# Two layer-norm halves beside the memory panels: the order of squares, outputs and weight splits changed

## The reference

```
h = _layer_norm_2(ALPHA * h + 0.5 * _swiglu(h, ffn1_w_gate, ffn1_w_up, ffn1_w_down), ln1_g, ln1_b)
proj = h @ w_in                       # first weights of the mixers: "wm"
...
m = _layer_norm_2(mem, mem_ln_g, mem_ln_b)
k = m @ wk                            # needs the memory only, not h
v = m @ wv
```

## Time and profile before

| | us |
|---|---|
| median of 3 runs | 2746.39 (2744.63 to 2747.12) |
| profiled execution | 2743.56 |
| its span, first to last instruction | 2741.8 |
| PE busy | 2685.2 (98%) |
| DVE busy | 1288.1 (47%) |
| ACT busy | 1019.1 (37%) |
| POOL busy | 278.1 (10%) |

### The profile page before, as it was taken

How to read it: one execution, slowest core, us unless ns; L and a number is a source line. 1 busy time by engine, 2 the same in 40 slices (tenths; PEclk the granted TensorE clock), 3 DMA queues, 4 the chain that set the end, 5 groups by cost and what they waited for, 6 DMA issues and landing times.

```text
span 2741.8 us, 39300 instructions
## 1 busy us (share of the span) xinstructions
PE 2685.2 (98%) x16240; PEld 2339.8 (85%) x16240; DVE 1288.1 (47%) x2198; ACT 1019.1 (37%) x1621; POOL 278.1 (10%) x350
## 2 busy tenths in 40 slices
PE   8999999999999999999999999999999999999997
PEld 7888999999987878788888988888888887888887
DVE  4664653334442423573344543435666655633333
ACT  4654433222332223352223432323557544522222
POOL 0000300001200000220000310002211130300002
PEclk9999999999999999999999999999999999999999
DMA  3111243222121212232222232222321212232320
GB/s 141 55 47 47 78 139 110 86 93 78 47 64 61 97 60 82 93 109 93 99 93 97 77 117 92 89 96 70 111 90 62 83 64 87 88 111 93 100 70 31
DMA packets 67682, 232.93 MB, mean 85 GB/s; under 512 B 9008, under 2 KB 11440, under 8 KB 67120
## 3 DMA queue, kind: packets, MB, share of 16 engines
q1 hardware_dynamic: 67504, 230.41, 25.5%
HBM read 228.25 MB, written 2.10 MB: 84 GB/s over the span
## 4 chain that ended last, share of the span: by engine, by line
PE 87%; DVE 4%; ACT 3%; POOL 2%; issue 2%; DMA 1%; SPq 0%; DVEq 0%; POOLq 0%; ACTq 0%
PE ps L595 76%; PE ps L898 2%; PE ps L1027 1%; POOL R L2725 1%; PE ps L605 1%; PE ps L797 1%; POOL S L2710 1%; PE ps L757 1%; PE ps L885 1%; ACT HT L1275 1%; DVE HT L1948 1%; DVE R L1955 1%; PE ps L1103 1%; PE ps L1124 1%; ACT HH L1236 0%
## 5 line engine op out<-in xcount | busy, mean ns | idle before, releaser
L595 PE MATMUL ps<-XH,WH 128*128 128x264 f32 (+2 forms) x1856 | 537.8, 332 | 13.2 <-POOL SCR L2760 7.8
L595 PE MATMUL ps<-XH,LENT 128*128 128x512 f32 (+2 forms) x2096 | 527.9, 342 | 3.1 <-DVE XL L1972 2.9
L595 PE MATMUL ps<-XL,WH 128*128 128x264 f32 (+2 forms) x1856 | 522.8, 324 | 0.0
L595 PE MATMUL ps<-XH,WL 128*128 128x264 f32 (+2 forms) x1856 | 522.2, 323 | 0.0
L595 PE MATMUL ps<-HH,LENT 128*128 128x264 f32 (+2 forms) x2220 | 490.7, 319 | 1.9 <-DVE LENT L1921 1.9
L1921 DVE TENSOR_TENSOR WL<-RAW,WH 128x1024 fp32r<-128x1024 f32 (+1 forms) x232 | 284.6, 1227 | 255.3 <-ACT WH L1231 255.2
L595 PEld LDWEIGHTS ps<-XH,LENT 128*128 128x128 f32 x2096 | 356.8, 189 | 53.3 <-DVE XL L1972 4.3
L595 PEld LDWEIGHTS ps<-HH,LENT 128*128 128x128 f32 x2220 | 361.3, 190 | 32.0 <-DVE LENT L1921 2.3
L595 PEld LDWEIGHTS ps<-XH,WH 128*128 128x128 f32 x1856 | 318.7, 189 | 56.8 <-issue 13.5
L595 PEld LDWEIGHTS ps<-XH,WL 128*128 128x128 f32 x1856 | 318.2, 189 | 28.1
L595 PEld LDWEIGHTS ps<-XL,WH 128*128 128x128 f32 x1856 | 318.3, 189 | 26.6
(11 more groups left out here) (222 smaller groups left out, 2670.3 us busy)
## 6 DMA issues: line engine op xcount, KB each, us to landing
RAW<-in_wf SPq DMA_DIRECT2D x128, 512.0 KB, 3.3
RAW<-in_wr SPq DMA_DIRECT2D x48, 512.0 KB, 3.3
RAW<-in_wg SPq DMA_DIRECT2D x44, 512.0 KB, 3.3
RAW<-in_wu SPq DMA_DIRECT2D x44, 512.0 KB, 3.3
RAW<-in_wd SPq DMA_DIRECT2D x32, 512.0 KB, 3.3
RAW<-in_we SPq DMA_DIRECT2D x24, 512.0 KB, 3.3
RAW<-in_wm SPq DMA_DIRECT2D x24, 512.0 KB, 3.2
RAW<-in_wro SPq DMA_DIRECT2D x16, 512.0 KB, 3.3
```

The costliest lines, as they stand in the source:

```text
L595: mm = e.matmul(o[:, to:to + m], wt, xt[:, k, c0 + a * m:c0 + (a + 1) * m], start=(n == 0 and j == 0), stop=(n == nk - 1 and j == 2))
```

## The change

It touches only `ln1`, the norm beside memory's panels. ACT and DVE get a function `norm_pair` that lays out both halves together; POOL's order is written to match, PE's places of total, stat and bcast are moved.

1. After the reciprocal of half 0, ACT and DVE run 8 steps instead of 5, so that one more residual (wd12 6) stands ahead of `mem_to_h`; behind `mem_to_h` one weight split is made instead of up to two, and then the last residual (wd12 7).
2. The centring and squares of half 1 come next, ahead of all outputs of half 0. Their first square stands after 2 steps of memory's panels instead of 16, and 2 steps instead of 1 follow each square.
3. The outputs of half 0 go to two free tiles of `TMP` (four places) instead of `HT`, since `HT` now holds half 1's squares. ACT issues two of them ahead of half 1's root, DVE three ahead of half 1's reciprocal. The remaining outputs of half 0 and then all of half 1 follow, each with 3 steps.
4. PE asks for half 1's total after 8 steps of memory's panels instead of 16, for its stat after 20 more instead of 17; the spread follows after 3 more, as before. Half 0's bank of the spread is kept until half 1's is given back.
5. POOL adds both halves' squares and all sums ahead of the outputs.

The core of the diff (the rest passes the functions along):

```diff
@@ -527,7 +527,14 @@
 
     def first_steps(ln, half):
 
-        return (6, 16 if ln == "ln1" else 8)[half]
+        return (6, 8)[half]
+
+    def normed_tile(ln, half, k, T):
+
+
+        if (ln, half) == ("ln1", 0):
+            return TMP[:, 2 + k % 4 // 2, HALF * (k % 2):HALF * (k % 2) + T]
+        return HT[:, T_SLOT[k], 0:T]
 
     def lead_turns(ln, half):
 
@@ -650,11 +657,15 @@
             w.wait_ge(*S.const["one"])
             e.matmul(o[:, 0:T], PART[:, :], sums, start=True, stop=True).then_inc(*S.total(ln, half))
             beside_mem = ln in ("ln1", "mem")
-            pump(17 if beside_mem else 18)
+            pump(20 if (ln, half) == ("ln1", 1) else 17 if beside_mem else 18)
             rstd((ln, half), [(HT[:, 1, 0:T], S.add_pool[(ln, half, 4)]), (HT[:, 2, 0:T], S.add_dve[(ln, half, 7)])],
                  T, (S.normed, ln, half, 7), pump, 3 if beside_mem else 4)
+            if (ln, half) == ("ln1", 0):
+                return
             pump(9)
             give(("bcast", (ln, half)))
+            if ln == "ln1":
+                give(("bcast", (ln, 0)))
 
...
+        def norm_pair(ln, T, c0, res, fill, other, meanwhile):
+
+            pump = pumping(fill)
+            norm_stats(ln, 0, T, res[0], pump, first_steps(ln, 0), normed[0])
+            pump(8)
+            meanwhile()
+            ah.upto(ah.panel + 5, 1)
+            drain(fill)
+            fill = other()
+            pump = pumping(fill)
+            norm_stats(ln, 1, T, res[1], pump, 2, None, lambda: [norm_out(ln, 0, T, c0, res[0], k, True)
+                                                                                  for k in range(2)])
+            for k in range(2, 9):
+                norm_out(ln, 0, T, c0, res[0], k, True)
+                pump(3)
+            for k in range(9):
+                norm_out(ln, 1, T, c0 + T, res[1], k, True)
+                pump(3)
+            normed[0] = (ln, 1)
+            return fill
+
@@ -1273,24 +1313,22 @@
                 if k == 7:
                     w.wait_ge(*S.add_dve[ln, half, 3])
                 e.activation(HT[:, SQ_SLOT[k], 0:T], res(k), ACT.Square).then_inc(*S.sq(ln, half, k))
-                pump(1)
+                pump(2 if (ln, half) == ("ln1", 1) else 1)
             pump(3)
+            if between:
+                between()
             root((ln, half), T, inv, LN_EPS)
-            pump(5)
-            if meanwhile:
-                meanwhile()
...
@@ -1642,7 +1682,6 @@
                 w.wait_ge(*S.r_out["mem", None, k])
                 w.wait_ge(*H_free("mem"))
                 to_h("mem", k, None, mem[:, k, :], 0, 256)
-            ah.upto(ah.panel + 5)
 
         def mem_panels(a, b, beside=()):
             for name, f in MEM[a:b]:
@@ -1939,7 +1978,41 @@
             roots = WIDE[key[1] % 2][:, a:b]
             e.reciprocal(roots, roots).then_inc(*S.recip(*key, b))
 
-        def layer_norm(ln, half, T, c, res, ready, pump, first, dst, meanwhile=None):
+        def layer_norm(ln, half, T, c, res, ready, pump, first, dst):
+            norm_stats(ln, half, T, res, ready, pump, first)
+            recip((ln, half), T)
+            pump(5)
+            for k in range(9):
+                norm_out(ln, half, T, c, res, k, dst)
+                pump(3)
+            norm_done(ln, half)
+
+        def norm_pair(ln, T, c0, res, ready, fill, other, meanwhile):
+
+            pump = pumping(fill)
+            norm_stats(ln, 0, T, res[0], ready[0], pump, first_steps(ln, 0))
+            recip((ln, 0), T)
+            pump(8)
+            meanwhile()
+            ah.upto(ah.panel + 5, 1)
+            drain(fill)
+            fill = other()
+            pump = pumping(fill)
+            norm_stats(ln, 1, T, res[1], ready[1], pump, 2)
+            for k in range(9):
+                if k == 3:
+                    recip((ln, 1), T)
+                norm_out(ln, 0, T, c0, res[0], k, True)
+                if k > 1:
+                    pump(3)
+            norm_done(ln, 0)
+            for k in range(9):
+                norm_out(ln, 1, T, c0 + T, res[1], k, True)
+                pump(3)
+            norm_done(ln, 1)
+            return fill
+
+        def norm_stats(ln, half, T, res, ready, pump, first):
             def add_square(k):
 
                 w.wait_ge(*S.sq[ln, half, k])
             add_square(6)
             add_square(7)
             pump(3)
-            recip((ln, half), T)
-            pump(5)
-            if meanwhile:
-                meanwhile()
-            spread = acc(("bcast", (ln, half)), 1)[:, 0:T]
-
-            def lower(k):
-                w.wait_ge(*S.x_hi[ln, half, k])
-                sig, event = out_mark(ln, half, k)
+
+        def norm_out(ln, half, T, c, res, k, dst):
+
+            if k < 8:
+                w.wait_ge(*S.bcast[ln, half])
+                w.wait_ge(*S.centre[ln, half, k])
+                reused = k - 4 if (ln, half) == ("ln1", 0) else k - 7
+                if reused >= 0:
+                    w.wait_ge(*S.r_out[ln, half, reused])
+                    if dst:
+                        w.wait_ge(*S.x_hi[ln, half, reused])
+                e.tensor_tensor(normed_tile(ln, half, k, T), res(k), acc(("bcast", (ln, half)), 1)[:, 0:T],
+                                ALU.mult).then_inc(*S.normed(ln, half, k))
+            if k > 0 and dst:
+                w.wait_ge(*S.x_hi[ln, half, k - 1])
+                sig, event = out_mark(ln, half, k - 1)
                 w.wait_ge(*sig[event])
-                e.tensor_tensor(XL[:, k, c:c + T], res(k), XH[:, k, c:c + T].bitcast(F32),
-                                ALU.subtract).then_inc(*S.x_lo(ln, half, k))
-            for k in range(9):
-                if k < 8:
-                    w.wait_ge(*S.bcast[ln, half])
...
@@ -2738,7 +2816,16 @@
             for m in ends(0):
                 sums(*m)
             second = ends(1)
-            if ln in ("ln1", "ln4"):
+            if ln == "ln1":
+                halves_of = [lambda k, c=c0 + half * T // 2: R[:, k, c:c + T // 2] for half in (0, 1)]
+                norm_adds(ln, 0, T // 2)
+                for m in second:
+                    sums(*m)
+                norm_adds(ln, 1, T // 2)
+                norm_out(ln, 0, T // 2, halves_of[0])
+                norm_out(ln, 1, T // 2, halves_of[1])
+                return
+            if ln == "ln4":
                 between = {-1: second[0:3], 0: second[3:4], 3: second[4:5]}
             else:
```

More of the change, by code:

```diff
@@ L1257, in wide_root, with layer_norm, norm_stats @@
                          scale=inv).then_inc(*S.root(*key))
-        def layer_norm(ln, half, T, c, res, pump, first, dst, meanwhile=None):
+        def layer_norm(ln, half, T, c, res, pump, first, dst):
+            norm_stats(ln, half, T, res, pump, first, normed[0])
+            pump(5)
+            for k in range(9):
+                norm_out(ln, half, T, c, res, k, dst)
+                pump(3)
+            normed[0] = (ln, half)
+        def norm_pair(ln, T, c0, res, fill, other, meanwhile):
[17 more added lines that the diff above has]
+            return fill
+        def norm_stats(ln, half, T, res, pump, first, before, between=None):
             inv = 1.0 / 1024
@@ L1275, in layer_norm @@
                 e.activation(HT[:, SQ_SLOT[k], 0:T], res(k), ACT.Square).then_inc(*S.sq(ln, half, k))
-                pump(1)
+                pump(2 if (ln, half) == ("ln1", 1) else 1)
             pump(3)
+            if between:
+                between()
             root((ln, half), T, inv, LN_EPS)
-            pump(5)
-            if meanwhile:
-                meanwhile()
-            for k in range(9):
[L1283 to L1293, removed]
+        def norm_out(ln, half, T, c, res, k, dst):
+            if k < 8 and dst:
+                w.wait_ge(*S.normed[ln, half, k])
+                w.wait_ge(*S.panel[final(AT[X_LAST[ln]])])
+                e.activation(XH[:, k, c:c + T], normed_tile(ln, half, k, T), ACT.Identity, bias=pcol(ln + "b", k),
+                             scale=pcol(ln + "g", k)).then_inc(*S.x_hi(ln, half, k))
+            if k < 8 and out_mark(ln, half, k)[0] is S.r_act:
+                w.wait_ge(*S.normed[ln, half, k])
+                e.activation(res(k), normed_tile(ln, half, k, T), ACT.Identity, bias=pcol(ln + "b", k),
+                             scale=pcol(ln + "g", k)).then_inc(*S.r_act(ln, half, k))
         def relu2(name, idx, c0, T, half):
@@ L1382, in down_norm @@
             fill = second()
-            for half in (0, 1):
+            if meanwhile:
+                fill = norm_pair(ln, T // 2, c0, [lambda k, c=c0 + half * T // 2: R[:, k, c:c + T // 2] for half in (0, 1)], fill,
+                                 other, meanwhile)
+            for half in () if meanwhile else (0, 1):
                 if half == 1:
@@ L1389, in down_norm @@
                     ah.most = AT[LEADS[ln][-1]] + 1
```

(20 more changed lines are left out.)

18 lines of the change are left out of this document (8 added, 10 removed).

## The result

| | before | after |
|---|---|---|
| median of 22 runs each | 2745.60 us | 2748.95 us |
| lowest to highest | 2741.70 to 2747.94 | 2743.26 to 2751.14 |
| ratio, 95% interval | | 1.0012 [1.0007, 1.0018] |
| profiled execution, span | 2743.56, 2741.8 | 2749.38, 2747.6 |

What follows compares the result with a forecast made beforehand. DVE and ACT, slower than PE with outputs between splits, pace the stretch; the early total (-4.3) and missing waits are paid back by outputs with splits and one more split: +0.3, 2743.56 to 2743.9 us; own range 2743 to 2750.5, overall 2740 to 2752.

Steps and rivals of the forecast that it cites:

- total of half 1: PE's total for the norm's half 1 starts at 1913.2 instead of 1917.47, 4.3 us earlier.
- DVE, split of wk2: DVE starts wk2's weight split at 1925.1, behind half 1's centring, two splits and added squares.
- to the splits of wk3, wv2, wv3, wm 0, wm 1: DVE's time from each weight split to the next, with outputs between: 3.25 us with one output, 0.77 per further output.
- end of the last low part: DVE ends half 1's last output at 1953.0, behind the second wm split; before, 1949.06, ahead of it.
- second wm panel: Its start on PE, the time to compare: 1953.9 against 1953.61 before; 1953 to 1955 named as a sign.
- two splits in the centring: wv0 and wv1 splits between half 1's centrings hold DVE 2.74 us each; lower bound 1.70 each gives -2.1 us.
- stops at its seventh and eighth step for the last low parts: PE in wm's first panel waits for DVE's last low parts; with one step (0.7) and hand-over it ends at 1953.9.
- PE's stops: PE's waits in the new order, from total to wm's first panel, add up to some 14 us.
- the half clock is then free: If PE falls to half clock near 1928, it costs nothing, since PE waits for the splits anyhow.
- handshakes overlap: Faster rival: ACT copies ahead, eight splits behind total lose 1.15 us each, 9.2 us: 2737.5; chance 0.16.
- second fall of the clock: Slower rival: PE's clock halves again on wm's panels, +4.9 to +5.5 us: 2752.2; chance 0.14.
- Memory port: POOL's second sum beside DVE's `mem_to_h` adds 0.45 us; by the skill's exclusion, its whole 0.73.

Runs made afterwards that it cites:

- e4: Kernel before with only half 1's last two residuals and sums moved ahead of all half 0 outputs: 2744.90 against 2743.81 us, ratio 1.0002.
- e8: Changed kernel with the last two V transpositions at steps 7 and 8 of wm's first panel, not 4 and 5: 2745.11 against the kernel before's 2744.40 us.
- e2: Changed kernel with the second wm panel's split behind all half 1 outputs on ACT and DVE: 2744.02 us against the kernel before's 2743.81.
- e1: Changed kernel with ACT's last V copy (wv3) moved ahead of the last output's high part: 2747.80 us against the kernel before's 2743.81.
- e3: Changed kernel with ACT copying the next weight panel one output after a panel's steps begin, not four: 2740.01 us against the kernel before's 2743.81.
- e6: Changed kernel with ACT's split copies earlier, last V copy earlier and second wm split behind all outputs: 2738.97 us against the kernel before's 2744.40.
- e7: The e6 kernel with half 1's root and reciprocal ahead of all half 0 outputs: 2739.15 us against the kernel before's 2744.40.
- e9: The e7 kernel with the first two V panels' transpositions in wk3 instead of wk2: 2743.39 us against the kernel before's 2744.40.
- e10: The e6 kernel with the first two V panels' transpositions in wk3 instead of wk2: 2740.15 us, ratio 0.9989 to the kernel before.

## Why the prediction was right, and where it was not

The forecast was +0.3 us within 2743 to 2750.5; the result is +3.3. Its steps, on the axis of before (times of after less 0.61):

| step | forecast | measured |
|---|---|---|
| `mem_to_h` | 1907.04, 3.75 long | 1907.06, 3.74 |
| total of half 1 | 1913.2 | 1913.22 |
| DVE, split of wk2 | 1925.1 | 1925.11 |
| to the splits of wk3, wv2, wv3, wm 0, wm 1 | 6.4, 4.9, 3.9, 4.9, 4.9 | 6.67, 4.87, 3.91, 4.88, 4.87 |
| end of the last low part | 1953.0 | 1953.15 |
| wm's first panel starts | 1946.7 | 1946.72 |
| second wm panel | 1953.9 | 1957.50 |

**Right: who paces, and that the early total is paid back.** The two splits in the centring held DVE for 2.64 and 2.65 us, near the 2.74 that I took for each: DVE went from its first centring to wk2's split in 11.19 us, forecast 11.25. At the other bound (1.70 a split) it would have been there 2.1 us earlier. e4 shows the other half: the early total by itself moves the stop to the next panel.

**Off in size: the end of wm's first panel.** The step that failed reads "stops at its seventh and eighth step for the last low parts [...] With one step (0.7) and hand-over it ends at 1953.9". I followed the data of the panel (the low parts) and forgot what else stands in it: a V transposition ahead of its fifth step, behind a copy that is queued on ACT behind the last output, and in a bank that the last output frees. The last term was to be 0.7 and hand-over; it measured 0.17 for the transposition and four steps, 4.42 us. Of the 3.6 us too many, three more steps at 0.70 are 2.1 and the half clock on the four steps 1.6 (4.42 less 2.80); small terms take back the rest. e8 takes the transposition out of the way and finds the forecast's distance; e2 and e1 show which queue and which bank. Of the signs that I had named, the second wm panel at 1953 to 1955 did not come true, for this reason. That the time still lies in the range is due to its width: the range had been set for the pace of the outputs, which was forecast well, and not for this.

**PE's stops.** Forecast 1.4, 1.0, 1.6, 0.4, 3, 2.3, 0.5, 2 and 1.8, some 14 us; measured 1.36, 0.75, 1.84, none, 1.43, 0.79, 0.30, 1.77 and 2.89, 11.1 us. The spread's is 1.43 only because the matmuls ahead of it ran at half clock there. In e8, where DVE's first low part comes at the same distance (29.27 against 29.25), PE was at full clock there and waited 2.95. That is the claim "the half clock is then free" seen directly: slow steps in place of a wait; the spread itself starts at the same distance in both (30.83 and 30.86). The first V transposition's 2.3 was too much by 1.5, and it cost nothing that shows: wm's first panel started where the forecast had it.

**The rival "handshakes overlap".** It was rightly given little: DVE's waits for ACT stayed, at 0.66 to 1.69 us. Its price of 9.2 us was too high. It was reckoned from the forecast's own 55.7 us of distance, which would make 46.5; made to happen, it gave 50.71 in e3 and, with the late gate moved as well, 48.74 in e6, 5.0 and 7.0 us less than 55.7. In e3 3.3 of the 10.7 us of waits remained.

**The rival "second fall of the clock".** It came in part: the clock did fall behind 1950, which I had named as a sign against me, and wm's panel paid 1.6 us for it. I had set the point from which it decides at some 10 us past 1954; it ended under 3 past. The mechanism was in the forecast, the stop ahead of it was not. Behind stops of 2.89 (after) and 1.93 us (e1) at that transposition the clock fell; behind 0.95 (e3) and 0.48 us (e2), and the 0.89 us of e8, the panel runs at 0.70 us a step. That is no rule yet: with the same stops in front (0.75 and 1.84 us, 0.77 and 1.87), wv1 started at half clock in after and at full clock in e8, and what decides there stays open.

**Memory port.** The second sum beside `mem_to_h` cost 0.44 (3.74 against 3.30), forecast 0.45. The Trainium skill (SBUF — State Buffer, "Who interferes with whom") has the two instructions exclude each other for the whole of one; by that it would have been 0.73. Measured is less, and so was the 0.45 of the low part in the earlier trace rows, which the prediction called agreement.

## What to carry to other kernels

When a chain is moved, list every instruction queued behind its last member and every buffer that it frees, not only its data: here the place of small transpositions and a bank cost 3.5 of the 3.9 us. Where two slower engines share a job, so that one waits for the other's half, put the first half ahead by one unit of other work. It pays where those two engines hold up the fastest one: the same edit shortened the stretch by 8.6 us in one order and by 0.8 in the other. Taking away a stop of the fastest engine gains little until the engines that feed it have slack: e4 and e7 took away stops of 2.8 and 2.5 us and got them back at PE's next waits.

## What the runs showed of the hardware

In these rows, where DVE's low parts and POOL's multiplications overlap, one of the two takes longer, now the one, now the other. POOL's and DVE's timelines after:

```profile
1927.39 1.09 POOL L2803 TENSOR_SCALAR R<-TMP,PV 128x256 f32<-128x256 f32 x2 [6.87 <-DVE TMP L2046]
1929.18 2.42 POOL L2803 TENSOR_SCALAR R<-TMP,PV 128x256 f32<-128x256 f32 x3 [0.70 <-DVE TMP L2046]
```

```profile
1928.05 0.70 DVE L2052 TENSOR_TENSOR XL<-R,XH 128x256 fp32r<-128x256 f32 x1 [0.43 <-POOL R L2803]
...
1929.94 0.43 DVE L2052 TENSOR_TENSOR XL<-R,XH 128x256 fp32r<-128x256 f32 x1
```

In the first group two take 0.55 each, and the low part at 1928.05, which overlaps the second, took 0.70 instead of 0.42. In the second group three take 0.81 each, and the low part at 1929.94, which lies wholly inside, took 0.43, its time alone. The forecast's 0.77 for an output held for the stretch, so this shift between the two cost nothing that can be seen.

A wait that the profile calls "issue" can be a wait for an accumulator bank, as e9 and e10 show (2.80 and 1.47 us): in both the matmul starts 0.10 us behind an instruction on another engine that the profile does not name as its releaser.
